# Two blocks of a transformer on one core: conditioning products as scaled row tiles on VectorE

## The chip, the core and the metric

The kernel runs on one core of a Trainium2 chip. The metric is the device time of one execution in microseconds (us). PE is TensorE, ACT is ScalarE, DVE is VectorE, SP is the engine whose queue issues nearly all transfers. Everything is in 32-bit floats.

## The reference, cut to what matters

Two models run one behind the other on 256 tokens of width 1024: first two layers (stick-breaking attention, dilated attention, feed-forward, a gated embedding), then two layers (MLA with pooling, GQA, a convolved feed-forward) that also see 256 context tokens. The second model is conditioned:

```
for i in range(2):
    ml = (silu(c) @ w_mod[i] + b_mod[i]).reshape(B, 6, 1, D)      # for the latents
    mc = (silu(c_ctx) @ w_mod[i] + b_mod[i]).reshape(6, D)        # for the context
    hl = modulate(xl, ml[:, 0], ml[:, 1]); hc = modulate(xc, mc[0], mc[1])
    ...                                                            # shifts, scales and gates 0 to 5
```

`w_mod` is 2 x 1024 x 6144, 50 MB: two vectors of 1024 times a matrix of 6144 columns, once for each layer. These products depend on `c` and `c_ctx` alone, so they can be made at any time before their use. The context leaves the kernel after layer 0, so of layer 1 its share is needed only for the first shift and scale (columns 0 to 2047).

## The kernel before, in words

**Linear layers.** Each is cut into weight chunks of at most 2048 elements a partition (1 MB), as a rule 8 blocks of 128 rows by 256 columns. There are 212 of them. A chunk is loaded by SP into one of three places of `raw`. ACT rounds it into `whi` (L1010, `split_high`), DVE makes the rest `wlo = raw - whi` (L1446, `split_low`), and PE adds three products: high by high, high by low, low by high (L647 is the line of every matmul). `whi` and `wlo` have three places (`SPLIT = 3`) too. So ACT may round chunk s+3 when PE has finished chunk s, DVE then makes its rest, and SP may load chunk s+6 into the place that this freed. Below, "the end of chunk s" is the time at which PE finishes it, and "position s" is the place in the order of ACT or DVE at which they handle the results of chunk s: evacuation, then the split of chunk s+3, then side work such as rotations (`rotate_pending`).

**Order of the linear layers.** `stick_qk` (8 chunks), `stick_v` (4), the attention phase `stick`, `stick_out` (4), `ff_in0` (16), `ff_out0` (16), `ple0`, `gate0`, then three times `dil_qk` (4) and `dil_v` (2), the phase `softmax`, `dil_out`, `ff_in1`, `ff_out1`, `ple1`, `gate1`; then with 512 tokens `mix_p`, `mix_c`, MLA, `mix_out`, `up00` (12), `down00` (8), `up01` (10), `down01` (8); then the second layer.

**The conditioning products.** `w_mod` is cut into 24 pieces of 512 columns by 1024 rows. A piece is two loads of 1 MB through the ring `raw`, without a split, in front of later chunks. PE makes `mod_products`: eight matmuls in full 32-bit with `cc` (the two vectors, as 2 of 24 columns, the others zero) as the fixed operand and 512 columns of the weights moving, four at a time in the four column groups of the array. The sums of a batch of up to 8 pieces gather in PSUM bank 7 (`MOD_BATCHES`). At the end of a batch ACT copies them (`mod_rows`, `modrow` lies in `lnv`), PE turns them with four matmuls (`mod_turn`), DVE adds the bias (`mod_keep`). The pieces stand in `stick_qk` (1), `stick` (7, one behind every second head), `mix_c` (2), `up00` (5), `down00` (3) and `up01` (6).

**Waits.** SP waits before each load for the user of the place's last content. A chunk whose last split is followed by a phase without matmul chunks can have that split put behind the phase (`late_splits`, `waiting_splits`), but not when the phase holds conditioning pieces.

Of the kernel before, what the change touches and what calls it, by code (L numbers as in the profile page):

```python
# [21 lines left out]
F32 = mybir.dt.float32  # L22
# [6 lines left out]
P = 128  # L29
D = 1024  # L30
# [19 lines left out]
MOD_ROWS = 24  # L50
MOD_BATCHES = (0, 8, 10, 12, 18, 24)
# [4 lines left out]
def constants():  # L56
# [20 lines left out]
    for q in range(4):  # L77
        for m in range(MOD_ROWS):
            select[32 * q + m, m] = 1.0
# [29 lines left out]
class Counting:  # L109
# [32 lines left out]
 ple_done max_ready fail_ready fail_summed stick_weights masked mod_rows mod_turned mod_kept gated_silu tiles_ready squares_folded half_moved""".split()  # L142


def build(nc, A, out, noted, dry_stop=None):
    C = Counting(noted)
    with ExitStack() as ctx:
        for f in FAMILIES:
            C.sems[f] = ctx.enter_context(nc.semaphore(f))
        landed = [ctx.enter_context(nc.semaphore(f"landed{i}")) for i in range(RAW)]  # L150
        loaded = {n: ctx.enter_context(nc.semaphore(f"loaded_{n}")) for n in ("squares", "rows", "freq", "pos", "x", "arena", "p")}
# [12 lines left out]
        h = sb("h", [P, KD, T2])  # L164
        u2 = sb("u2", [P, 2, KD, T2], F32R)
        uh, ul = u2[:, 0, :, :], u2[:, 1, :, :]
# [5 lines left out]
        cos1 = sb("cos1", [P, S])  # L172
        sin1 = sb("sin1", [P, S])
# [6 lines left out]
        cc = sb("cc", [P, KD, 2 * MOD_ROWS - 2])  # L180
        small = sb("small", [P, 64])
        ident, ones, negtri, negones, perm1, perm_m, perm_g, past, select = (squares[:, j, :] for j in range(9))
        select = select[:, 0:MOD_ROWS]
# [51 lines left out]
        pin, ph_, pl_ = y[:, 0:2, S:T2], uh[:, 0:2, S:T2], ul[:, 0:2, S:T2]  # L235
# [6 lines left out]
        csil = arena("csil", [P, 2, 512], 28 * K)  # L242

# [33 lines left out]
        for l in range(2):  # L277
# [3 lines left out]
            if l == 0:  # L281
# [3 lines left out]
                phase("stick", n_mods=7)  # L285
# [16 lines left out]
            linear(f"ple{l}", A["w_ple"][l], 2, [(0, D)], S, "ple", xin=("u", 0), tok0=S)  # L302
# [51 lines left out]
        mod_after = dict(stick_qk=(4,), mix_c=(0, 1), up00=(1, 3, 5, 7, 9), down00=(0, 1, 2), up01=(1, 2, 3, 5, 6, 7))  # L354
        own_chunks, behind, mod_n = [], {}, 0
        for p in phases:
            p["mods"] = {}
            places = range(p["n_mods"]) if "n_mods" in p else mod_after.get(p.get("name"), ())
            for g, grp in enumerate(p.get("groups", [()])):
                own_chunks += grp  # L360
                for place in places:
                    if "groups" in p and place != g:
                        continue
                    l, c = divmod(mod_n, 12)
                    pair = [dict(job=p, mod=(l, c, half), kn=4, C=512,
                                 src=A["w_mod_2"][l][half * 512:(half + 1) * 512, c * 512:(c + 1) * 512]) for half in range(2)]
                    behind.setdefault(len(own_chunks) + SPLIT - (2 if "groups" in p else 1), []).extend(pair)
                    p["mods"][place] = (mod_n, pair)
                    mod_n += 1
        assert mod_n == 24 or dry_stop is not None  # L370
        order = []
        for n, c in enumerate(own_chunks):
            order += [c] + behind.get(n, [])
        chunks = order
        n_split = 0
        for r, c in enumerate(chunks):
            c["r"] = r
            if "mod" not in c:
                c["s"] = n_split
                n_split += 1  # L380
        splits = [c for c in chunks if "s" in c]
# [1542 lines left out]
```

## Time and profile before

| | us |
|---|---|
| median of 3 runs (lowest, highest) | 1920.99 (1912.36, 1924.91) |
| the profiled execution: its own time | 1921.89 |
| the profiled execution: span | 1919.8 |
| PE busy in the span | 1820.7 |
| DVE busy | 1049.7 |
| ACT busy | 874.1 |
| mean granted clock of PE | 0.975 of full speed |
| loaded from memory | 262.08 MB |

The span is the time from the first to the last instruction; the kernel's own time holds 2.1 us more. A matmul's record has a modelled end, so the distance between starts says more than the duration. Records of full 32-bit matmuls come in two per matmul.

### The profile page before, as it was taken

To read this page: it belongs to the slowest core of one execution; us is meant where nothing else is said; L and a number is where in the kernel's file an instruction comes from. 1 tells how busy PE (TensorE), PEld (TensorE's weight loads), DVE (VectorE), ACT (ScalarE), POOL (GpSimd) and SP (SyncE) were. 2 spreads that over 40 slices of the span, in tenths; PEclk is the share of its full clock that TensorE was granted. 3 is DMA by queue.
4 is the path that set the end of the run, shared out by engine and by line. 5 is a ranking of instruction groups with operands and counts; after the bars stand their busy time and mean duration, and the time that the engine had idled before them with its cause. 6 is when DMAs were issued, how large, how long until landed. Compare 5 with 4: busy or idle time off the path is not lost.

```text
span 1919.8 us, 25364 instructions
## 1 busy us (share of the span) xinstructions
PE 1820.7 (95%) x10222; PEld 1496.4 (78%) x10222; DVE 1049.7 (55%) x1370; ACT 874.1 (46%) x1108; POOL 0.2 (0%) x4
## 2 busy tenths in 40 slices
PE   6989999989999899989988999999999988999998
PEld 4857788988887788887756686777877867789997
DVE  4444775466554776464456644444233555667764
ACT  5455454354435454345445625332222344565552
POOL 0000000000000000000000000000000000000000
PEclk9989999999989999999998999999999999999999
DMA  5766365534520456533313023544565224035551
GB/s 189 238 213 212 116 194 193 184 110 144 169 95 5 133 178 196 180 105 102 117 36 114 1 88 110 176 153 148 181 219 186 89 81 133 1 101 186 190 182 68
DMA packets 227895, 264.76 MB, mean 138 GB/s; under 512 B 4672, under 2 KB 196163, under 8 KB 227779
## 3 DMA queue, kind: packets, MB, share of 16 engines
q1 hardware_dynamic: 226114, 258.89, 41.1%
q10 hardware_dynamic: 1664, 4.26, 0.7%
q8 instruction: 81, 1.33, 0.3%
q14 instruction: 36, 0.29, 0.0%
HBM read 262.08 MB, written 1.05 MB: 137 GB/s over the span
## 4 chain that ended last, share of the span: by engine, by line
PE 83%; DVE 8%; ACT 7%; issue 1%; DMA 1%; DVEq 0%; ACTq 0%
PE ps L647 81%; ACT y L1267 2%; PE ps L944 2%; ACT u L1270 1%; DVE wlo L1446 1%; ACT whi L1010 1%; DVE y L1714 1%; DVE u L1707 1%; DVE y L1731 1%; DVE rstd L1629 1%; DVE rstd L1631 1%; DMA xin<-in_ctx 1%; DVE h L1735 0%; DVE h L1517 0%; ACT lnv L1085 0%
## 5 line engine op out<-in xcount | busy, mean ns | idle before, releaser
L647 PE MATMUL ps<-u,whi 128*128 128x512 f32 (+2 forms) x3408 | 896.8, 346 | 34.3 <-DVE u L1707 16.4
L647 PEld LDWEIGHTS ps<-u,whi 128*128 128x128 f32 (+1 forms) x3408 | 590.9, 191 | 141.5 <-DVE u L1707 26.0
L647 PE MATMUL ps<-u,wlo 128*128 128x256 f32 (+1 forms) x2084 | 645.6, 310 | 0.0
L1446 DVE TENSOR_TENSOR wlo<-raw,whi 128x2048 fp32r<-128x2048 f32 (+6 forms) x212 | 454.0, 2142 | 339.5 <-ACT whi L1010 335.6
L1010 ACT ACTIVATE whi<-raw 128x2048 fp32r<-128x2048 f32 (+6 forms) x212 | 380.7, 1796 | 230.2 <-PE ps L647 197.9
L647 PEld LDWEIGHTS ps<-u,wlo 128*128 128x128 f32 x2084 | 398.4, 191 | 20.9
L647 PE MATMUL ps<-hid,whi 128*128 128x512 f32 (+1 forms) x1212 | 352.6, 363 | 0.0
L647 PE MATMUL ps<-hid,wlo 128*128 128x256 f32 (+1 forms) x864 | 261.6, 303 | 0.0
L647 PEld LDWEIGHTS ps<-hid,whi 128*128 128x128 f32 x1212 | 216.4, 189 | 39.8 <-DVE y L1492 2.5
L647 PEld LDWEIGHTS ps<-hid,wlo 128*128 128x128 f32 x864 | 163.4, 189 | 6.9
L647 PE MATMUL ps<-squares 128*128 128x256 f32 (+1 forms) x396 | 95.0, 390 | 5.7 <-issue 3.2
L647 PEld LDWEIGHTS ps<-squares 128*128 128x128 f32 x396 | 76.3, 195 | 19.8 <-issue 9.6
L1192 ACT ACTIVATE cacc<-ps,convv 128x512 f32<-128x512 f32 (+1 forms) x44 | 29.6, 673 | 121.6 <-PE ps L647 120.8
L1536 DVE SCALAR_TENSOR_TENSOR cacc<-ps,convv,cacc 128x510 f32<-128x510 f32 (+1 forms) x44 | 27.1, 616 | 91.8 <-ACT cacc L1192 89.3
L647 PE MATMUL ps<-whi,u 128*128 128x512 f32 (+1 forms) x224 | 65.7, 374 | 0.0
L1202 ACT ACTIVATE csil<-cacc 128x512 f32<-128x512 f32 (+1 forms) x44 | 23.1, 525 | 91.1 <-PE ps L647 88.6
L1109 ACT ACTIVATE work<-ps 128x512 f32<-128x512 f32 x38 | 22.8, 599 | 90.3 <-PE ps L647 90.2
L1379 ACT ACTIVATE pt<-ps 128x512 f32<-128x512 f32 (+2 forms) x72 | 37.1, 515 | 53.4 <-PE ps L944 52.6
L1707 DVE TENSOR_TENSOR u<-y,u 128x256 fp32r<-128x256 f32 (+1 forms) x80 | 40.4, 505 | 26.5 <-ACT u L1270 21.5
L1549 DVE TENSOR_TENSOR csil<-ps,csil 128x512 f32<-128x512 f32 (+1 forms) x44 | 24.6, 559 | 51.9 <-ACT csil L1202 48.3
L944 PEld LDWEIGHTS ps<-squares,pr 128*128 128x128 f32 x232 | 28.8, 149 | 29.3 <-issue 15.6
L1270 ACT ACTIVATE u<-y 128x256 fp32r<-128x256 f32 (+1 forms) x80 | 38.5, 482 | 22.4 <-DVE y L1714 19.7
(211 smaller groups left out, 1578.7 us busy)
## 6 DMA issues: line engine op xcount, KB each, us to landing
raw<-in_w_mod SPq DMA_DIRECT2D x48, 1024.0 KB, 5.5
raw<-in_ffn_w_up SPq DMA_DIRECT2D x44, 1024.0 KB, 5.1
raw<-in_w_ff_in SPq DMA_DIRECT2D x32, 1024.0 KB, 5.3
raw<-in_w_ff_out SPq DMA_DIRECT2D x32, 1024.0 KB, 5.1
raw<-in_w_in_dil SPq DMA_DIRECT2D x18, 1024.0 KB, 5.1
raw<-in_w_in_sb SPq DMA_DIRECT2D x12, 1024.0 KB, 6.0
raw<-in_w_ple_gate SPq DMA_DIRECT2D x8, 1024.0 KB, 5.2
raw<-in_ffn_w_down SPq DMA_DIRECT2D x8, 896.0 KB, 5.0
```

What stands on the lines that cost most here:

```text
L647: return pe.matmul(out_, lhsT, rhs, start=start, stop=stop, skip_group_check=True)
L944: last = pe.transpose(ps[:, (4 + k // 4) if wide else 4 + n % 2, (k % 4) * P:(k % 4 + 1) * P], pr[:, n % 2, k * P:(k + 1) * P], ident)
L1010: nc.scalar.activation(whi[:, s % SPLIT, 0:n], raw[:, c["r"] % RAW, 0:n], ACT.Copy).then_inc(*up("weights_high", s))
L1192: nc.scalar.activation(cacc[:, j, 0:T], A_[:, j, :], ACT.Identity, bias=convv[:, l, 66 + f:67 + f], scale=convv[:, l, 22 + f:23 + f]).then ...
L1202: nc.scalar.activation(csil[:, j, 0:T], cacc[:, j, 0:T], ACT.Silu).then_inc(*up("gated_silu", (i, g - 1, j)))
L1267: nc.scalar.activation(y[:, k, sl], y[:, k, sl], ACT.Identity, bias=mod_at(l, which, k, s_), scale=mod_at(l, which + 1, k, s_)).then_inc(* ...
L1270: nc.scalar.activation(dst[:, k_, 0:p["T"]], y[:, p.get("s0", 0) + k, 0:p["T"]], ACT.Copy).then_inc(*up("operand_high", (i, k)))
L1379: nc.scalar.activation(pt[:, n % 2, c0:c0 + w], ps[:, (4 + c0 // 512) if u["mask"] is not None else 4 + n % 2, 0:w], ACT.Copy).then_inc(*u ...
L1446: nc.vector.tensor_tensor(wlo[:, s % SPLIT, 0:n], raw[:, c["r"] % RAW, 0:n], whi[:, s % SPLIT, 0:n].bitcast(F32), ALU.subtract).then_inc(* ...
L1536: nc.vector.scalar_tensor_tensor(a[:, :, 1:S], x[:, :, 0:S - 1], convv[:, l, f:f + 1], a[:, :, 1:S], ALU.mult, ALU.add).then_inc(*up("vect ...
L1549: nc.vector.tensor_tensor(csil[:, j, 0:T], A_[:, j, :], csil[:, j, 0:T], ALU.mult).then_inc(*up("group_read_v", (i, g, j)))
L1707: nc.vector.tensor_tensor((cl if c else ul)[:, k_, 0:T], y[:, s0 + k, 0:T], (ch if c else uh)[:, k_, 0:T].bitcast(F32), ALU.subtract).then ...
```

## The change

`w_mod` no longer goes through PE as a product. It is cut into 96 row tiles of 128 rows by 1024 columns (0.5 MB, two transfers of 256 KB each). DVE multiplies a tile by one number per partition (the entry of the vector for that row) and adds it to a running sum of 128 by 1024: `tensor_scalar` for the first of 8 tiles, `scalar_tensor_tensor` for the other seven, once for each vector. When the eight tiles of a set are in, PE adds the sum over its 128 partitions with a column of ones (`unit_row`), four matmuls of 512 columns in four column groups. ACT copies, PE turns, DVE adds the bias as before.

There are 10 sets: 0 to 7 have 1024 columns and both vectors (8 tiles, 16 DVE instructions each), 8 and 9 have 2048 columns and the first vector alone (16 tiles, 16 DVE instructions each). The tiles have five places of their own, three in the unused half of `u2` (sets 0 to 4) and two in the arena (sets 5 to 9); the ring `raw` now carries chunks alone, and `late_splits` no longer looks at pieces.

A planner places tiles by chunk (`share`). Worked out from its rules, the tiles lie at these positions of DVE, and PE adds the set behind the chunk named:

| set | tiles at positions | PE adds it behind chunk |
|---|---|---|
| 0 | 1 to 8 (`stick_qk`, first of `stick_v`), 1 each | 12 (`stick_out`) |
| 1 | 13, 14 (`stick_out`), 32 to 37 (`ff_out0`), 1 each | 38 |
| 2 | 39 to 43 (`ff_out0`), 53 to 55 (`dil_qk0`), 1 each | 56 |
| 3 | 57 to 64 (`dil_v0`, `dil_qk1`, `dil_v1`), 1 each | 65 (`dil_qk2`) |
| 4 | 66 to 70 (`dil_qk2`, `dil_v2`), 91 to 93 (`ff_out1`), 1 each | 94 |
| 5 | 130 to 133 (`up00`), 2 each | 134 |
| 6 | 135 to 138 (`up00`), 2 each | 139 |
| 7 | 140, 141 (`up00`), 142, 143 (`down00`), 2 each | 144 |
| 8 | 145 to 149 (`down00`), 150 to 152 (`up01`), 2 each | 153 |
| 9 | 154 to 159 (`up01`), 160, 161 (`down01`), 2 each | 162 |

The tile for a place is loaded by SP in front of the chunk load seven positions behind the place's last use, once DVE has taken the old tile. The turn stands two chunks behind the addition. The core of the diff:

```diff
@@ SP: loads
                 for c in chunks:
                     r = c["r"]
+                    for m in mod_dma.get(r, ()):
+                        if m["earlier"]:
+                            sp.wait_ge(*at("mod_taken", m["earlier"]["n"]))
+                        elif m["slot"] >= 3:
+                            sp.wait_ge(*at("attended", (mla_i, 31)))
+                        for unit in range(2):
+                            c0 = (m["c"] + unit) * 512
+                            src = A["w_mod_2"][m["set"]["l"]][m["k"] * P:(m["k"] + 1) * P, c0:c0 + 512]
+                            sp.dma_start(mod_weights(m)[:, 2 * unit:2 * unit + 2, :], src.rearrange("p (b c) -> p b c", b=2)).then_inc(mod_landed[m["slot"]], 16)
                     if r >= RAW:
-                        o = chunks[r - RAW]
-                        if "s" in o:
-                            sp.wait_ge(*at("weights_low", o["s"]))
-                        else:
-                            sp.wait_ge(*at("weights_used", ("mod", o["r"])))
+                        sp.wait_ge(*at("weights_low", r - RAW))
@@ PE: behind each chunk
-                    if g - 1 in p["mods"]:
-                        mod_turn(p["mods"][g - 1][0])
-                    if g in p["mods"]:
-                        mod_products(*p["mods"][g])
+                        mod_turn(c["r"] - 2)
+                        mod_products(c["r"])
...
+            def mod_products(r):
+                st = mod_place.get(r)
+                if st is None:
                     return
+                pe.wait_ge(*at("mod_taken", ("set", st["i"])))
+                for q in range(4):
+                    a, unit = (q % 2, q // 2) if len(st["vecs"]) == 2 else (q // 2, q % 2)
+                    last = mm(ps[32 * q:32 * q + 32, 7, :], unit_row[:, :], mod_sum(st, a)[:, 2 * unit:2 * unit + 2, :], True, True)
+                last.then_inc(*up("mod_added", st["i"]))
@@ DVE: behind the split of each position, ahead of the rotations
+            def mod_scaled(r):
+                for m in mod_steps.get(r, ()):
+                    k, st = m["k"], m["set"]
+                    if k == 0 and m["c"] == st["c0"] and st["i"] > 0:
+                        dve.wait_ge(*at("mod_added", st["i"] - 1))
+                    dve.wait_ge(mod_landed[m["slot"]], 32 * (m["nth"] + 1))
+                    for v in st["vecs"]:
+                        total = mod_sum(st, v if len(st["vecs"]) == 2 else (m["c"] - st["c0"]) // 2)
+                        dve.wait_ge(*own())
+                        if k == 0:
+                            nc.vector.tensor_scalar(total, mod_weights(m), cc[:, k, v:v + 1], None, ALU.mult).then_inc(*up("mod_taken", m["n"]))
+                        else:
+                            nc.vector.scalar_tensor_tensor(total, mod_weights(m), cc[:, k, v:v + 1], total, ALU.mult, ALU.add).then_inc(
+                                *up("mod_taken", m["n"]))
@@ late splits
-            if p["kind"] != "linear" or phases[p["i"] + 1]["kind"] in ("linear", "final", "dump") or phases[p["i"] + 1]["mods"]:
+            if p["kind"] != "linear" or phases[p["i"] + 1]["kind"] in ("linear", "final", "dump") :
                 return [], []
```

Beside this the embedding input `p` moves to other places (`pin0` and half of `rstd`, low part in `ul[:, 6:8]`), and the two rotation tables share one buffer.

## Rows read from the trace of the kernel before

**Rows 1.** Page: busy time by engine; the chain's shares by engine.
```profile
PE 1820.7 (95%) x10222; PEld 1496.4 (78%) x10222; DVE 1049.7 (55%) x1370; ACT 874.1 (46%) x1108; POOL 0.2 (0%) x4
...
PE 83%; DVE 8%; ACT 7%; issue 1%; DMA 1%; DVEq 0%; ACTq 0%
```
**Rows 2.** Waits: waiting line, releaser; us in total, times, longest.
```profile
PE ps L647 <- DVE u L1707: 16.4, 34, 3.2
```
**Rows 3.** Groups by form: xcount, busy us, mean ns, idle before; PE and DVE.
```profile
L647 PE MATMUL ps<-raw,cc 128*24 128x512 f32 x384 | 46.0, 597 | 0.0
...
L647 PE MATMUL ps<-squares,lnv 128*128 128x24 f32 x40 | 4.9, 261 | 0.0
...
L1446 DVE TENSOR_TENSOR wlo<-raw,whi 128x2048 fp32r<-128x2048 f32 x174 | 398.9, 2293 | 270.6 <-ACT whi L1010 267.8
...
L1714 DVE SCALAR_TENSOR_TENSOR y<-h,vec,rstd 128x256 f32<-128x256 f32 x48 | 23.3, 485 | 16.3 <-ACT rstd L1088 14.5 <-DVE wlo L1446 0.2
...
L1536 DVE SCALAR_TENSOR_TENSOR cacc<-ps,convv,cacc 128x510 f32<-128x510 f32 x22 | 16.5, 749 | 79.9 <-ACT cacc L1192 78.7
...
L1848 DVE TENSOR_SCALAR pr<-pr,small 128x512 f32<-128x512 f32 x32 | 15.6, 486 | 1.1
...
L1848 DVE TENSOR_SCALAR pr<-pr,small 128x768 f32<-128x768 f32 x8 | 5.0, 620 | 0.5 <-DVE small L1846 0.2
```
**Rows 4.** Timeline of PE in `up00`: start, us, operation.
```profile
1208.18 0.39 PE L647 MATMUL ps<-u,wlo 128*128 128x512 f32 x1
1208.50 1.92 PE L647 MATMUL ps<-raw,cc 128*24 128x512 f32 x16
1210.35 0.73 PE L647 MATMUL ps<-u,whi 128*128 128x512 f32 x2
```
**Rows 5.** Timeline of ACT in `stick`: one exponential per head.
```profile
129.48 0.49 ACT L1345 ACTIVATE sba<-ps 128x384 f32<-128x384 f32 x1 [1.84 <-PE ps L647]
132.19 0.49 ACT L1345 ACTIVATE sba<-ps 128x384 f32<-128x384 f32 x1 [0.47 <-PE ps L647]
136.75 0.49 ACT L1345 ACTIVATE sba<-ps 128x384 f32<-128x384 f32 x1 [1.84 <-PE ps L647]
```
**Rows 6.** Timeline of DVE and of PE at the start of `stick`.
```profile
107.80 2.29 DVE L1446 TENSOR_TENSOR wlo<-raw,whi 128x2048 fp32r<-128x2048 f32 x1 [4.23 <-ACT whi L1010]
...
111.27 2.08 PE L647 MATMUL ps<-sbf,squares 128*128 128x256 f32 x6 [3.83 <-DVE sbf L1788]
```
**Rows 7.** Windows: length, PE, PEld, DVE, ACT, POOL busy; clock, DMA share, GB/s.
```profile
108.00:112.00 4.00, 0.73 (x2) 0.64 (x3) 3.72 (x5) 2.93 (x6) 0.00 (x0) 0.50 0.18 28
...
144.00:152.00 8.00, 8.00 (x49) 4.86 (x49) 3.41 (x8) 5.04 (x11) 0.00 (x0) 1.00 0.86 300
```
**Rows 8.** Timeline of DVE in `ff_out0`: two splits in a row.
```profile
335.87 2.29 DVE L1446 TENSOR_TENSOR wlo<-raw,whi 128x2048 fp32r<-128x2048 f32 x1 [3.25 <-ACT whi L1010]
341.42 2.29 DVE L1446 TENSOR_TENSOR wlo<-raw,whi 128x2048 fp32r<-128x2048 f32 x1 [3.25 <-ACT whi L1010]
```
**Rows 9.** Timeline of DVE in `dil_qk0`, and at the start of its softmax.
```profile
471.13 2.29 DVE L1446 TENSOR_TENSOR wlo<-raw,whi 128x2048 fp32r<-128x2048 f32 x1 [2.07 <-ACT whi L1010]
473.52 0.69 DVE L1581 TENSOR_TENSOR work<-ps,sin 128x512 f32<-128x512 f32 x1
...
477.74 2.29 DVE L1446 TENSOR_TENSOR wlo<-raw,whi 128x2048 fp32r<-128x2048 f32 x1 [2.06 <-ACT whi L1010]
...
564.76 0.56 DVE L1831 CUSTOM_DVE_ANT_0 sm<-ps,masks 128x384 f32<-128x384 f32 x1 [5.29 <-PE ps L647]
```
**Rows 10.** Timeline of ACT and DVE in `up00`, behind an even chunk.
```profile
1197.73 1.60 ACT L1192 ACTIVATE cacc<-ps,convv 128x512 f32<-128x512 f32 x2 [9.37 <-PE ps L647]
...
1203.41 2.29 DVE L1446 TENSOR_TENSOR wlo<-raw,whi 128x2048 fp32r<-128x2048 f32 x1
```
**Rows 11.** Transfers by line: count, KB each, median us to landing.
```profile
raw<-in_w_mod SPq DMA_DIRECT2D x48, 1024.0 KB, 5.5
...
ropeg<-in_const_rope ACTq DMA_DIRECT2D x1, 256.0 KB, 2.8
```

More of the change, by code:

```diff
@@ L350, in build @@
                 p["idle"] = 11 if phases[i - 1]["T"] == T2 else 7
[L354 to L375, printed above, removed]
-        for r, c in enumerate(chunks):
[L377 to L381, printed above, removed]
+        for r, c in enumerate(chunks):
+            c["r"] = c["s"] = r
+        mla_i = max((i for i, p in enumerate(phases) if p.get("what") == "mla"), default=None)
@@ new lines, in jobs_at, with unbroken @@
+        def jobs_at(name):
+            return min((c["r"] for c in chunks if c["job"]["name"] == name), default=len(chunks))
+        def unbroken(p, q):
+            between = phases[p["i"]:q["i"]]
+            return all(o["kind"] == "linear" and "stat" not in o for o in between)
+        sets = []
+        for a, b in [(n, n + 2) for n in range(0, 16, 2)] + [(16, 20), (20, 24)]:
+            sets.append(dict(i=len(sets), l=a // 12, c0=a % 12, c1=a % 12 + b - a, vecs=(0, 1) if b - a == 2 else (0,)))
@@ new lines, in build @@
+        share = dict(stick_qk=1, stick_v=2, stick_out=1, ff_out0=2, dil_qk0=1, dil_v0=1, dil_qk1=1, dil_v1=1,
+                     dil_qk2=1, dil_v2=1, ff_out1=2, up00=4, down00=4, up01=4, down01=4)
+        mod_steps, mod_place, mod_dma, mod_tiles = {}, {}, {}, []
+        todo = [(st, c, k) for st in sets for c in range(st["c0"], st["c1"], 2) for k in range(KD)]
+        free_at, early = 1, 0
+        for ck in chunks:
+            r, job = ck["r"], ck["job"]
+            room = share.get(job["name"], 0)
+            if job.get("stat") and ck["g"] + 1 == len(job["groups"]):
+                room = 0
+            while room > 0 and todo and r >= free_at and (todo[0][0]["i"] < 5) == (r < jobs_at("mix_p")):
+                st, c, k = todo[0]
+                n = len(mod_tiles)
+                early += st["i"] < 5
+                slot = n % 3 if st["i"] < 5 else 3 + (n - early) % 2
+                earlier = [m for m in mod_tiles if m["slot"] == slot]
+                if earlier and earlier[-1]["r"] == r:
+                    break
+                todo.pop(0)
+                m = dict(n=n, set=st, c=c, k=k, slot=slot, nth=len(earlier), earlier=earlier[-1] if earlier else None, r=r)
+                mod_tiles.append(m)
+                mod_steps.setdefault(r, []).append(m)
+                mod_dma.setdefault((earlier[-1]["r"] if earlier else r - 3) + 7, []).append(m)
+                room -= len(st["vecs"])
+                if not todo or todo[0][0] is not st:
+                    place = r + 1
+                    while place + 3 < len(chunks) and not unbroken(chunks[place]["job"], chunks[place + 3]["job"]):
+                        place += 1
+                    mod_place[place] = st
+                    free_at = place + 1
@@ L385, in build @@
+        assert not todo or dry_stop is not None
+        splits = chunks
         for p in phases:
@@ L632, in build @@
             if p.get("name", "").startswith("ff_in"):
-                p["loads"] = [(pin[:, :, :], A["p"][int(p["name"][5:]), 0].rearrange("(t p) d -> p t d", p=P))]
+                p["loads"] = [(pin[t], A["p"][int(p["name"][5:]), 0][t * P:(t + 1) * P, :]) for t in range(2)]
             for _ in p.get("loads", ()):
```

130 lines of the change are left out of this document (64 added, 66 removed).

## The prediction

> **What bounds the kernel now.** I read the page first: PE is busy 1820.7 of 1919.8 us and makes 83% of the chain that ended last; DVE is busy 55% of the span [rows 1]. Then the waits: the longest wait of PE's matmuls in total is 16 us, on the first operand tiles of a layer, not on weights [rows 2]. So in the linear layers every us taken off PE's queue is a us of the span, and VectorE has slack on average. But PE, ACT and DVE are coupled at every chunk, so the question is where DVE is late once it carries the tiles. The profiled execution took 1921.9 us, 0.9 over the median of 1921.0; all sums are against it. A difference under 1% (19 us) can't be told from no change here.
>
> **What leaves PE.** The 24 pieces make 46 us of PE in all [rows 3]. In `up00` a piece starts at 1208.50, and the next chunk's matmul starts 2.17 us after the last one of the chunk before [rows 4]. A chunk is 48 matmuls in 10.7 us (from 1197.73, where ACT is released by its predecessor [rows 10], to the piece's start less a matmul), 0.22 each; so the piece costs 1.94 us. 17 pieces stand in linear layers: **-33.0**. The turns: 40 records, 4.9 us, five turns, about 0.9 us of path each [rows 3]; four are in linear layers: **-3.6**.
>
> Seven pieces are in `stick`. A head that has no piece ahead of it takes 132.19-129.48 = 2.71 us, one that has takes 4.56 [rows 5]. The difference, 1.85, is nearly the whole piece, but ACT had only 0.47 us of idle in the short head, so when all heads are short ACT is nearly the bound as well; 1.83 each: **-12.8**. The fifth turn and its `mod_keep` stand between the last two heads: **-1.0**. And `stick` no longer holds pieces, so the split of chunk 14 goes behind it: DVE's 2.29 us of it end at 110.09, and PE starts the first head's sums at 111.27 after 3.83 us of waiting for DVE [rows 6]: **-2.3**. Behind `stick` that split is hidden by chunks 12 and 13; without that cover it costs 4 us. The clock fell to 0.50 in that wait [rows 7]. A shorter wait may keep it: a gain between 0 and 2.5 us (five or six short heads of matmuls at half speed), taken as 0, since PE still waits.
>
> **What comes to PE.** Ten additions of four matmuls where a piece had eight: half of 1.94, say 1.0, and ten turns of 0.9: **+19**. Ten ACT copies of 0.6 us for five, and twice the small `mod_keep`, lie in slack: 0. Without waits the sum is -33.7.
>
> **What comes to DVE.** A multiply-add with a per-partition number took 485 ns for 256 and 749 ns for 510 elements, so 1.04 ns an element and, as an estimate, 1.28 us for 1024. `tensor_scalar` took 486 and 620 ns for 512 and 768: 0.75 us for 1024 [rows 3]. 140 of the first and 20 of the second: 195 us, DVE to 65%. A tile for both vectors is 2.65 us with gaps. The Trainium skill, VectorE: DVE Perf Modes, section on the fixed extra latency, gives (N+151)/0.96 for a plain tensor-tensor, 1.22 us here; its rule would shorten the waits below by some 10%, and leaves the forecast where it is.
>
> Now each addition. PE reaches it one chunk after the last tile's position began. DVE begins there with the split of three chunks ahead, for which ACT must first round.
> - `ff_out0`, `ff_out1`: splits are 5.55 us apart, and DVE idles 3.25 us between them [rows 8]. The split begins 2.0 us after the chunk's end (ACT's rounding), ends at 4.3, the tile at 6.95; PE is there at 5.55. Sets 1 and 4 wait 1.4 each: **+2.8**.
> - `dil_qk`: chunks end 6.6 us apart; DVE has 2.29 of split and three rotations of 0.73 [rows 9], with a tile 7.15 us. DVE falls behind by 0.55 each time, beyond the wait for ACT of about 2.9 us that starts every position. Set 2 (three positions, the first without rotation): DVE ends at 476.6, PE is there at 474.85: **+1.75**. Set 3 has eight positions in a row. Following them one by one (split when ACT is ready or DVE free, tile, rotation of the chunk before) DVE ends 4.5 us after chunk 65: **+4.5**. That is a stop as long as the one that lost the clock at 108 us [rows 7]; half speed for 4 us costs **+2**.
> - Set 4's five positions lead up to the dilated softmax. DVE's first instruction of it is at 564.76, after 5.29 us of idle [rows 9]. With two rotations, five tiles (one of them short) and the splits moved along, DVE is free at 567.9: **+3.2**.
> - Tiles at 13 and 14 delay the last copy of `stick_out`, on which the norm waits: **+1.2**.
> - `up00`, two tiles of 5.3 us: an even chunk's DVE work ran to 8.0 us behind the chunk's end (1203.41+2.29-1197.73 [rows 10]), with tiles 13.3, where the next chunk ends at 10.8. The odd one has some 3 us less and gives part of it back. Followed chunk by chunk the ends lie 0.9 (set 5), 2.4 (set 6) and, into the shorter chunks of `down00`, 3.1 us (set 7) behind PE: **+6.4**. Sets 8 and 9 have half the DVE work: 0 and **+0.75**. Set 0: two phases of time, 0.
> The split itself (`wlo`) is never late: it has three chunks of lead, 16 us, and DVE lags at most 5.
>
> **Transfers.** The same 50 MB go in 192 transfers of 256 KB past the chunk loads on SP's queue. SP waits for `mod_taken` before each tile; the load queued behind it waits for a split that DVE makes later than that tile, so the wait costs nothing. In `ff_out0` and `stick_qk` a chunk and a tile, 1.57 MB, must come in 5.55 us: 283 GB/s. `stick` moved 300 GB/s for 8 us with PE never idle [rows 7]. Cost 0, with the second rival as the bound. The moves of `p` and of the tables: 0, the same work in other places, hidden under `ff_out`; uncovered 3 us.
>
> **Sum.** -33.7 + 2.8 + 1.75 + 4.5 + 2 + 3.2 + 1.2 + 6.4 + 0.75 = -11.1: 1921.9 - 11.1 = **1911 us**. The gain is two thirds eaten by PE waiting for DVE.
>
> **Rivals.**
> - *DVE is in time.* If a multiply-add is cheaper than I extrapolate, or the lags don't add up, only the -33.7 remains: 1888; with the clock kept at 108 us, 1886. For it: three chunks of lead, DVE at 65%. Against it: PE stands at the addition without any lead, one chunk after the last tile, and the 1.4 us in `ff_out0` need no lag. It decides from a tile below 1.3 us. Chance 0.25.
> - *The transfers bind; slower.* A 1 MB load lands in 5.5 us (190 GB/s alone), 256 KB in 2.8 us, half the time for a quarter of the bytes [rows 11]. Place: the 40 early positions with a tile. If no more than 230 GB/s come through, 1.57 MB take 6.8 us: 24 positions of 5.55 us lose 1.3, 16 of 6.6 lose 0.2, together +34: 1945. At 190 GB/s it is 24 x 2.7 + 16 x 1.65 = +91: 2002. It decides below 283 GB/s. Against it: 300 GB/s in `stick`, in loads of 1 MB. Chance 0.11. The Trainium skill, DMA: Bandwidth & Descriptors, section Bandwidth, asks for transfers of 1 MiB or more for three quarters of the peak (341 GB/s at 1 MB, 138 at 64 KB); by that rule the change goes this way.
> - *The pieces filled time that is lost anyway* (ACT's order in `stick`, waits that move elsewhere), and DVE's lags also delay evacuations: gain under 5 us, 1917 to 1930. Chance 0.19.
> - Forecast, 1902 to 1917: 0.45.
>
> **Range.** 1889 to 1929 leaves out the transfers' case and the far end of the first rival. The likeliest case's own range is 1902 to 1917. Faster by over 1% means below 1902: the first rival and the low edge of the forecast, 0.32. Slower than 1940: the transfers and a little of the third, 0.12. Within: 0.56.
>
> **What would show it.** The profile after should show about 80 records of additions (128 x 32) where 384 of `raw`,`cc` stood, DVE's multiply-adds at 1.28 us x140, DVE near 1245 us; a wait of PE on them of 15 us in all, the longest at `dil_qk2` about 4 to 5 us, and a clock dip there; `stick` shorter by 16 us, all heads at 2.7; the first split at `stick`'s start gone. No wait of DVE on a tile's transfer. I am wrong if PE's wait on DVE there is under 5 us (first rival), or if DVE or ACT wait on DMA for more than 10 us (second).

## The result: same at 2%, on the slow side, and the forecast was for faster

The changed kernel took **1928.86 us** (median of 20, 1919.06 to 1944.23), the kernel before 1920.53 (20 runs, 1912.0 to 1927.34): ratio 1.0057, 95% interval 1.0033 to 1.0081. Forecast was 1911. Eight more executions, in a second comparison, gave 1.0069 (1.0038 to 1.0099). The profiled execution, 1943.85 us (span 1942.0), is one of the slowest; two later profiled ones had spans of 1921.3 and 1937.0, so three traces of each kernel are used below. The median of all 29 executions of the changed kernel is 1930.95 us. One of the twelve executions of before_fill_more took 2412.84 us at a mean granted clock of 0.70; it is left out of that run's ratio.

The page of the changed kernel, then the matmuls' waits on VectorE, answering [rows 1, 2]; columns as there.

```profile
PE 1816.4 (94%) x9958; PEld 1509.7 (78%) x9958; DVE 1245.1 (64%) x1539; ACT 877.2 (45%) x1113; POOL 0.2 (0%) x4
...
PE 72%; DVE 16%; ACT 8%; issue 2%; DMA 1%; DVEq 0%; ACTq 0%; SPq 0%
```
```profile
PE ps L685 <- DVE u L1756: 16.5, 35, 3.2
...
PE ps L685 <- DVE y L1695: 9.6, 4, 4.7
PE ps L685 <- DVE work L1695: 6.9, 3, 3.1
...
PE ps L685 <- DVE small L1878: 4.3, 1, 4.3
```

TensorE lost its 24 pieces and is busy only 4 us less; VectorE's share of the chain doubled. The three new lines are the waits for the sets' sums (L1695) and for VectorE at the start of the dilated softmax. A fourth, 2.2 us, stands at the last set. The new work by form, answering [rows 3]:

```profile
L1695 DVE SCALAR_TENSOR_TENSOR y<-idle_half,cc,y 128x1024 f32<-128x1024 f32 x70 | 89.9, 1284 | 4.9
...
L1693 DVE TENSOR_SCALAR y<-idle_half,cc 128x1024 f32<-128x1024 f32 x10 | 7.5, 753 | 0.8
```
```profile
L685 PE MATMUL ps<-squares,lnv 128*128 128x4 f32 x80 | 9.5, 242 | 0.0
...
L685 PE MATMUL ps<-y,unit_row 128*32 128x512 f32 x40 | 7.1, 786 | 9.6 <-DVE y L1695 9.6
```

1.28 us and 0.75 us, as extrapolated. The two splits of `ff_out0` [rows 8] now have a tile between them, and the first addition behind comes late, TensorE's line third:

```profile
333.02 2.29 DVE L1476 TENSOR_TENSOR wlo<-raw,whi 128x2048 fp32r<-128x2048 f32 x1 [0.54 <-ACT whi L1041]
335.42 2.60 DVE L1695 SCALAR_TENSOR_TENSOR y<-idle_half,cc,y 128x1024 f32<-128x1024 f32 x2
338.66 2.29 DVE L1476 TENSOR_TENSOR wlo<-raw,whi 128x2048 fp32r<-128x2048 f32 x1 [0.64 <-ACT whi L1041]
```
```profile
338.07 1.06 PE L685 MATMUL ps<-y,unit_row 128*32 128x512 f32 x8 [1.45 <-DVE y L1695]
...
544.54 1.93 PE L685 MATMUL ps<-y,unit_row 128*32 128x512 f32 x8 [4.66 <-DVE y L1695]
...
586.51 2.07 PE L685 MATMUL ps<-qk 64*128 64x256 f32 x4 [4.29 <-DVE small L1878]
```

The second line is set 3, the third the dilated softmax. There VectorE still worked off tiles when its first maximum was due, where it had idled 5.29 us [rows 9]:

```profile
580.40 5.31 DVE L1695 SCALAR_TENSOR_TENSOR y<-idle_half,cc,y 128x1024 f32<-128x1024 f32 x4
585.89 0.56 DVE L1878 CUSTOM_DVE_ANT_0 sm<-ps,masks 128x384 f32<-128x384 f32 x1 [0.18 <-DVE y L1695]
```

At the sticks the wait is down from 3.83 to 2.09 us [rows 6], but the exponentials [rows 5] show the first heads 3.58, 5.05 and 3.49 us apart and only the later ones at the forecast 2.7, by turns 2.84 and 2.59. (The kernel before had 3.58, 5.24 and 2.72 there: its first heads were as long.)

```profile
108.70 1.65 PE L685 MATMUL ps<-sbf,squares 128*128 128x256 f32 x4 [2.09 <-DVE sbf L1839]
```
```profile
110.81 0.49 ACT L1377 ACTIVATE sba<-ps 128x384 f32<-128x384 f32 x1 [1.52 <-PE ps L685]
114.39 0.49 ACT L1377 ACTIVATE sba<-ps 128x384 f32<-128x384 f32 x1 [1.34 <-PE ps L685]
119.44 0.49 ACT L1377 ACTIVATE sba<-ps 128x384 f32<-128x384 f32 x1 [2.81 <-PE ps L685]
122.93 0.49 ACT L1377 ACTIVATE sba<-ps 128x384 f32<-128x384 f32 x1 [1.25 <-PE ps L685]
125.77 0.49 ACT L1377 ACTIVATE sba<-ps 128x384 f32<-128x384 f32 x1
```

The windows say why (columns as in [rows 7]; the granted clock follows POOL): sticks, the norm behind `stick_out`, dilated softmax, latent attention. The second fence is the kernel before at the same work.

```profile
108.00:124.00 16.00, 15.30 (x50) 11.11 (x51) 6.24 (x14) 8.19 (x18) 0.00 (x0) 0.59 0.00 1
184.00:200.00 16.00, 11.73 (x39) 9.19 (x38) 10.30 (x20) 4.04 (x7) 0.00 (x0) 0.79 0.28 91
...
580.00:612.00 32.00, 26.72 (x115) 20.15 (x116) 16.37 (x41) 10.93 (x24) 0.00 (x0) 0.68 0.16 50
1052.00:1088.00 36.00, 34.82 (x105) 21.51 (x105) 18.76 (x66) 14.25 (x45) 0.00 (x0) 0.53 0.06 21
```
```profile
108.00:124.00 16.00, 12.73 (x55) 8.48 (x56) 7.30 (x12) 8.57 (x18) 0.00 (x0) 0.68 0.40 137
564.00:596.00 32.00, 31.46 (x166) 23.71 (x165) 15.09 (x48) 14.65 (x33) 0.00 (x0) 0.79 0.00 1
1028.00:1064.00 36.00, 34.18 (x135) 20.67 (x136) 24.45 (x78) 19.30 (x57) 0.00 (x0) 0.76 0.12 40
```

With the levels 2.4 and 1.2 GHz, a mean clock of c over a window of T us holds (1-c)/0.5 x T us at half clock: 20.5 us in the changed kernel's softmax against 13.4, 33.8 in its latent attention against 17.3. Over the whole span (mean clocks 0.961, 0.971, 0.961 against 0.975, 0.975, 0.976) it is 151, 111 and 151 us against 96, 96 and 92.

The extra half clock is not spread evenly. Read in windows of 1 us and summed by the stages of the table below, it is (mean of three traces, changed against before): start to `stick_out` 15.9 against 15.9 us, join 4.6 against 0, dilated stages 27.3 against 12.5, latent attention 29.6 against 15.9, `up00` to `down01` 11.0 against 0.7. The other stages differ by under 3 us each.

The transfers did no harm (count, KB, median us to landing, answering [rows 11]); in the whole trace VectorE waited 2.0 us for a tile.

```profile
modw<-in_w_mod SPq DMA_DIRECT2D x112, 256.0 KB, 4.0
idle_half<-in_w_mod SPq DMA_DIRECT2D x80, 256.0 KB, 3.4
```

**Where the time went.** Stage lengths between the records of ScalarE that write `rstd` (us). First column: the kernel before, mean of three traces; the others are differences to it. "Changed" is the mean of three traces, the experiments one trace each.

| stage | before | forecast | changed | fill | add_later | combined_mla | before_all_fill |
|---|---|---|---|---|---|---|---|
| start to stick_out, its norm | 171.4 | -14.9 | -10.5 | -15.0 | -11.1 | -16.4 | -4.9 |
| join | 9.9 | 0 | +1.6 | 0.0 | +2.5 | 0.0 | 0.0 |
| ff_in0, ff_out0 | 188.7 | +3.3 | +5.0 | +5.2 | +3.3 | +1.0 | +1.7 |
| ple0, gate0, norms | 52.0 | 0 | +1.0 | +0.2 | +1.1 | +0.2 | +1.5 |
| dilated stages | 188.9 | +15.3 | +20.4 | +10.1 | +13.3 | +2.7 | -3.6 |
| join, ff_in1, ff_out1 | 205.8 | +3.3 | +1.9 | +1.8 | +0.4 | +2.3 | +0.5 |
| to mix_c | 142.7 | -4.8 | -3.9 | -3.6 | -5.1 | -3.0 | 0.0 |
| latent attention, mix_out | 168.0 | 0 | +5.9 | +9.4 | +0.6 | -3.4 | -4.5 |
| up00 to down01 | 410.0 | -13.2 | -7.4 | -8.8 | -21.6 | -20.6 | -0.3 |
| rest | 345.2 | 0 | -0.7 | -0.9 | -0.3 | -0.9 | -0.8 |
| sum | 1882.7 | -11 | +13.3 | -1.5 | -16.8 | -38.0 | -10.4 |

The forecast's column is its terms put to their stages (an addition with its turn 1.9, a piece -1.94, waits as listed). The miss by these traces is 24 us, by the medians 18. fill's and before_fill_more's traces have the long stretch in the latent attention told of below, so their sums lie above their medians. The miss sits in the sticks with the norm behind them and the join (6), the dilated stages (5), the latent attention (6, code that the change does not touch) and `up00` to `down01` (6).

### The profile page after: what moved, and what is told of

Same layout as the page of the kernel before. It is cut to its first block, busy times and chain, and to the rows that moved or that the text cites. A ratio compares the mean times of both kernels' runs of the same rounds, so it can differ in the third digit from the quotient of the medians.

```text
span 1942.0 us, 25257 instructions
## 1 busy us (share of the span) xinstructions
PE 1816.4 (94%) x9958; PEld 1509.7 (78%) x9958; DVE 1245.1 (64%) x1539; ACT 877.2 (45%) x1113; POOL 0.2 (0%) x4
## 4 chain that ended last, share of the span: by engine, by line
PE 72%; DVE 16%; ACT 8%; issue 2%; DMA 1%; DVEq 0%; ACTq 0%; SPq 0%
PE ps L685 70%; DVE wlo L1476 4%; DVE y L1695 2%; ACT y L1299 2%; ACT whi L1041 2%; PE ps L975 2%; ACT u L1302 1%; DVE work L1695 1%; DVE sq L1695 1%; DVE y L1763 1%; DVE u L1756 1%; DVE rstd L1659 1%; DVE rstd L1661 1%; DMA xin<-in_ctx 1%; DVE h L1547 0%
## 5 line engine op out<-in xcount | busy, mean ns | idle before, releaser
L685 PEld LDWEIGHTS ps<-squares 128*128 128x128 f32 x396 | 78.5, 201 | 20.4 <-issue 9.1
L1695 DVE SCALAR_TENSOR_TENSOR y<-idle_half,cc,y 128x1024 f32<-128x1024 f32 x70 | 89.9, 1284 | 4.9
L1223 ACT ACTIVATE cacc<-ps,convv 128x512 f32<-128x512 f32 (+1 forms) x44 | 29.6, 673 | 113.3 <-PE ps L685 112.5
L1566 DVE SCALAR_TENSOR_TENSOR cacc<-ps,convv,cacc 128x510 f32<-128x510 f32 (+1 forms) x44 | 27.1, 616 | 50.2 <-ACT cacc L1223 47.5
L685 PE MATMUL ps<-sq,squares 128*128 128x256 f32 (+1 forms) x108 | 39.6, 494 | 9.7 <-DVE qg L1622 6.1
```

The source lines that it names most:

```text
L685: return pe.matmul(out_, lhsT, rhs, start=start, stop=stop, skip_group_check=True)
L1223: nc.scalar.activation(cacc[:, j, 0:T], A_[:, j, :], ACT.Identity, bias=convv[:, l, 66 + f:67 + f], scale=convv[:, l, 22 + f:23 + f]).then ...
L1566: nc.vector.scalar_tensor_tensor(a[:, :, 1:S], x[:, :, 0:S - 1], convv[:, l, f:f + 1], a[:, :, 1:S], ALU.mult, ALU.add).then_inc(*up("vect ...
L1695: nc.vector.scalar_tensor_tensor(total, mod_weights(m), cc[:, k, v:v + 1], total, ALU.mult, ALU.add).then_inc(*up("mod_taken", m["n"]))
```

## The experiments

**Theory.** The waits for VectorE came as forecast; what was mis-sized is TensorE's clock: behind idle time of 2 to 5 us at the stage ends and additions it falls to half, and 3 to 34 us of work follow at that speed. **Rivals:** the waits alone are the loss; or the clock is luck.

**Both kernels again** (no edit).

> The kernel before, unchanged, profiled a second time. Question: how much of the change in the low-clock time between the two traces (before 0.975 of the span at full clock, after 0.961) is chance. Every theory: time 1.000 of before. Clock theory (gaps that VectorE makes at stage ends let TensorE's clock fall): the low-clock stretches of this kernel repeat, with none at the third set's place (dil_qk2) and the dilated softmax at full clock again by 580 us; mean clock 0.973 to 0.977. Chance theory (the low stretches in the changed kernel are luck): a stretch that the first profile did not have turns up here too, and the mean clock differs from 0.975 by over 0.005.

> The changed kernel, unchanged, profiled a second time. Every theory: 1.004 of before. Clock theory: clock below 0.9 again at 540 to 550 us (third set's addition) and at 580 to 610 us (start of the dilated softmax), behind waits of TensorE of over 2 us for VectorE, and 8 us of half clock more than in the kernel before behind the sticks. Whatever low stretch it does not show again, the latent attention's from 1052 to 1086 us above all, is chance and no part of the loss. Chance theory: the low stretches sit elsewhere.

> The kernel before a third time: half clock in the latent attention for 17.1 and 13.7 us in the first two. If its length is luck with the same odds in both kernels, a stretch of over 20 us should be seen in about one of three executions; if not, it stays at 13 to 17 us and the changed kernel loses there for a reason of its own.

> The changed kernel a third time, for one more trace of the latent attention, code that the change does not touch: half clock there for 34.1 and 10.2 us in the first two. If its length is luck, it lies between 10 and 34 us, and the rest of the trace agrees with the other two within 3 us in every stretch.

Measured: before_again 1921.45 us, ratio 0.9999 (0.9977 to 1.0022), mean clock 0.975; after_again 1932.27 us, 1.0069 (1.0038 to 1.0099), profiled at 0.971; before_third 1923.83, after_third 1938.82 (one execution each). Behind the third set and in the dilated softmax there was half clock in all three traces of the changed kernel, and the softmax's stretch was 17 to 21 us against 10 to 14 before. That is not luck. The latent attention is another matter; its windows in after_again and after_third:

```profile
1040.00:1076.00 36.00, 32.39 (x141) 19.60 (x139) 26.08 (x78) 20.90 (x58) 0.00 (x0) 0.86 0.18 59
```
```profile
1040.00:1076.00 36.00, 32.61 (x101) 20.19 (x101) 20.88 (x62) 16.18 (x44) 0.00 (x0) 0.59 0.18 59
```

0.86 and 0.59 are 10 and 30 us at half clock in the window at the same instructions behind the same waits. That stage's length differs by 10.4 us between the three traces, the largest part of why the changed kernel's executions lie 25 us apart; the rest agreed within 4.5 us in each stage (3 was expected), the most in the sticks and in `up00` to `down01`. The kernel before showed 17, 14 and 14.

**fill**: TensorE kept busy ahead of its waits, VectorE's work and moments untouched.

```
+ fill(n): n matmuls ones x squares, 256 columns, into a bank nobody reads
  mod_products:        + fill({1: 3, 2: 4, 3: 10, 6: 5, 7: 6}.get(set, 0)) ahead of the wait
  sticks, first head:  + fill(4)
  behind stick_out:    - idle(5)  + idle(12)
  dilated softmax:     + fill(9) ahead of the third scores
```

> The changed kernel with matmuls that nobody reads put ahead of the waits for VectorE: 3, 4, 10, 5 and 6 ahead of the additions of sets 1, 2, 3, 6, 7, 9 at the start of the dilated softmax, 4 at the first head of the sticks, and 12 in place of 5 behind stick_out. VectorE's work and the moment at which its results come are untouched; TensorE is only busy instead of idle before them. Clock theory: the clock stays at full speed behind the third set and in the dilated softmax, and the low stretch behind the sticks is shorter: 8 to 17 us less than the changed kernel, 0.995 to 1.000 of before. Rival (the waits themselves are the whole loss, the clock is chance): no change from the changed kernel or up to 2 us more, 1.004 to 1.005.

Measured: 1912.16 us, 0.9961 (0.9939 to 0.9982), 20.1 us less than after_again's 1932.27 in the same comparison, 16.7 less than the first comparison's 1928.86. Its sticks, set 3 and dilated softmax ran at full clock:

```profile
104.00:120.00 16.00, 14.94 (x80) 11.60 (x81) 6.81 (x15) 12.43 (x25) 0.00 (x0) 1.00 0.19 63
...
540.00:548.00 8.00, 8.00 (x65) 7.52 (x63) 3.17 (x3) 3.20 (x4) 0.00 (x0) 1.00 0.01 2
568.00:600.00 32.00, 30.28 (x190) 23.69 (x190) 21.34 (x55) 16.17 (x35) 0.00 (x0) 1.00 0.16 50
```

From the first `q,k` matmul to the last exponential the sticks took 44.3 us, where the changed kernel needed 50.0, 49.1 and 47.5. The table puts 10 of the gain in the dilated stages, 4.5 in the sticks, 1.6 in the join. In `up00` to `down01` the fillers gave 1.4 us, though half clock there went from 11.0 to 6.6 us: most of the loss in that stretch was the waits themselves, and there the rival is right.

**add_later**: the additions one chunk further behind.

```
  if last tile of the set:  place = r + 1 (moved on to an unbroken place)
+     if place == r + 1:
+         place += 1      (and moved on in the same way)
```

> The changed kernel with TensorE's four additions of each set one chunk later, so that VectorE, which ends a set's last tile late, has a whole chunk more; tiles and loads stay where they are. The waits of TensorE for the sets' sums (9.6 us in all, largest 4.66 at the third set) should go to under 1 us. Clock theory: the waits and the clock dips behind them both go, 11 to 16 us less than the changed kernel, so 0.995 to 0.999 of before; the slow stretch at the dilated softmax's start stays, since VectorE is late there for its tiles and not for the addition. Rival (VectorE's backlog only moves on: TensorE waits for the operand or the split instead): 0 to 4 us less, 1.002 to 1.004 of before, and the wait stands at another line at the same time.

Measured: 1907.41 us, **0.992** (0.989 to 0.9951), 25 us under after_again (21 under the first comparison's median) and more than either theory gave. No wait of TensorE for L1695's sums is left in its trace; the other waits that grew did so by 1.8 us in all, 1.1 of them for `qk`. `up00` to `down01` is 21.6 us shorter than before; the forecast without its waits says 13.2+7.15 = 20.4. The softmax's wait stayed, as expected:

```profile
576.13 2.50 PE L689 MATMUL ps<-qk 64*128 64x256 f32 x5 [4.61 <-DVE small L1882]
```

**tiles_off_dil_v2**: on top of add_later.

```
- dil_v2=1
+ dil_v2=0
```

> The kernel add_later with the two tiles (four passes of VectorE, 5.1 us) of dil_v2 moved into ff_out1, the share of dil_v2 set to 0. Term tested: the start of the dilated softmax, priced +3.2 us, where TensorE now waits 4.6 us for VectorE and then runs 17 to 20 us at half clock against 10 to 14 in the kernel before. VectorE-backlog theory: the wait is back at 0.4 to 0.6 us and the half clock at 10 to 14 us, 5 to 9 us less than add_later: 0.987 to 0.990 of before. Rival (the four additions and turns moved in front of the softmax make it late, not the tiles): the wait stays over 3 us, and 0.991 to 0.993.

Measured: 1897.1 us, 0.9867 (0.9836 to 0.9898), 10 us under add_later, of which its trace shows 4.7 in the dilated stages. What the rest is, its trace, the slowest of its six executions, does not show. The wait came of the tiles, not of the additions:

```profile
570.05 1.41 PE L689 MATMUL ps<-qk 64*128 64x256 f32 x4 [0.43 <-DVE small L1882]
```

The half clock behind stayed at 17 us, longer than the 10 to 14 expected.

**before_stick_fill and before_fill_more**: the same fillers in the kernel before.

```
  sticks, first head:  + fill(4)          (before_fill_more: + fill(8))
  dilated softmax:     (before_fill_more: + fill(3) ahead of the scores, + fill(1) ahead of the third)
```

> The kernel BEFORE, with only four matmuls that nobody reads at the first head of the sticks, where TensorE waits 3.83 us for VectorE (rows 6). It asks whether the 5.6 us that the fillers brought in the changed kernel's sticks belong to the change at all. Clock theory (the half clock for 10.2 us from 108 us on is set by that idle time, in either kernel): no low stretch at 108 to 124 us, the sticks 4 to 6 us shorter, 0.997 to 0.998 of before. Rival (only the changed kernel loses clock there): no change, 0.9995 to 1.001.

> The kernel BEFORE with eight unread matmuls at the first head (four left 1.91 us of idle and a half clock of 6.8 us), and 3 and 1 of them at the start of the dilated softmax, in front of the waits of 1.21 and 0.43 us. It asks what the fillers alone bring to the kernel before, and so what part of combined's gain is not of the moved products. Clock theory: no half clock at 108 to 124 us and at 565 to 590 us; the sticks' part from 58.2 us to 55 to 57, the softmax from 46.8 us to 43 to 45: 4 to 7 us less, 0.9965 to 0.998 of before. Rival (in the kernel before the heads and the softmax are bound by other engines even at half clock): 0 to 2 us, 0.999 to 1.001.

Measured: before_stick_fill 1923.04 us, 1.0007 (0.999 to 1.0024). The theory's gain did not come, but the test is inconclusive: four fillers left a wait of 1.91 us in front of the first sums, and the clock fell as before, for 7 us instead of 10.

```profile
108.59 1.99 PE L647 MATMUL ps<-squares 128*128 128x256 f32 x8
112.50 1.70 PE L647 MATMUL ps<-sbf,squares 128*128 128x256 f32 x6 [1.91 <-DVE sbf L1795]
```

before_fill_more: 1920.32 us, 0.9988 (0.9969 to 1.0007), less than expected. In its trace the sticks ran at full clock and took 57.7 us instead of 61.0, 61.7 and 61.2; the dilated stages were 3.7 us shorter. But most of what it gained there this trace lost in the latent attention (5.9 us), where the kernel before now had 31 us of half clock too (windows of the sticks and of the latent attention):

```profile
106.00:122.00 16.00, 15.15 (x87) 11.03 (x88) 7.52 (x13) 11.61 (x20) 0.00 (x0) 1.00 0.61 212
...
1020.00:1056.00 36.00, 33.02 (x104) 20.45 (x103) 21.38 (x63) 15.67 (x45) 0.00 (x0) 0.57 0.18 59
```

So the long stretch does not need the moved products. The sticks at full clock, first and last exponential, in before_fill_more and then in fill (51.2 and 39.5 us):

```profile
113.22 0.49 ACT L1356 ACTIVATE sba<-ps 128x384 f32<-128x384 f32 x1 [1.28 <-PE ps L647]
...
164.38 0.49 ACT L1356 ACTIVATE sba<-ps 128x384 f32<-128x384 f32 x1 [0.69 <-PE ps L647]
```
```profile
109.70 0.49 ACT L1387 ACTIVATE sba<-ps 128x384 f32<-128x384 f32 x1 [0.59 <-PE ps L685]
...
149.20 0.49 ACT L1387 ACTIVATE sba<-ps 128x384 f32<-128x384 f32 x1 [1.68 <-PE ps L685]
```

**after_mla_fill**, **combined** and **combined_mla**.

```
after_mla_fill (on the changed kernel):
  pool_w:          + fill(3)
  latent softmax:  + fill(4) ahead of the first scores
combined (on tiles_off_dil_v2): the two above, sticks + fill(4), behind stick_out idle(12),
  dilated softmax + fill(3) ahead of the scores, + fill(1) ahead of the third
combined_mla (on combined): pool_w - fill(3); latent softmax fill(4) becomes fill(5),
  + fill(4) ahead of the first turn, + fill(2) ahead of the second
```

> The changed kernel with matmuls that nobody reads only in the latent attention: 3 ahead of the pool's weights and 4 ahead of the first scores, in front of waits of 1.6 and 2.1 us that both kernels have. The changed kernel's executions lie anywhere from 1919 to 1944 us, the kernel before's only from 1912 to 1930; in one trace of the changed kernel the clock stood at half for 34 us from 1053 us on, in another for 10 us at 1046. Theory: this stretch is the spread, and it is chance, given by the same idle time in both kernels: with the fillers the low stretch is 0 to 3.4 us, no execution is over 1932, the median is 1920 to 1925, 0.9995 to 1.002 of before. Rival (the spread comes from elsewhere, from the changed kernel's own waits): the median stays at 1927 to 1932 and the spread over 20 us.

> All together: the additions one chunk later, no tiles in dil_v2, and matmuls that nobody reads ahead of the waits at the first head (4), behind stick_out (12 in place of 5), ahead of the dilated softmax (3 and 1), of the pool's weights (3) and of the latent scores (4). Clock theory, summed from the parts: add_later 1907.4, less 7 for dil_v2's tiles, 5.6 for the sticks, 1.5 for the join, 5 for the dilated softmax's clock, 6 for the latent attention's: 1882, 0.978 to 0.984 of before. Rival (a stretch held at full clock lets the next one fall instead, so that the parts do not add up): 1890 to 1900, 0.985 to 0.990.

> combined without the 3 matmuls ahead of the pool's weights (the wait of 1.62 us stood there as before), but with 5 ahead of the first latent scores and 4 and 2 ahead of the first two turns, where TensorE waited 1.39 and 0.53 us. Theory: the half clock in the latent attention (10 to 34 us long in every trace so far) is set at these waits, and goes: 5 to 9 us less than combined, 1882 to 1886, 0.980 to 0.981 of before. Rival (it comes of the few columns per us that TensorE has in this softmax, not of the idle before): it stays over 10 us, 1889 to 1895, 0.984.

Measured: after_mla_fill 1934.89 us, 1.0063 (1.0042 to 1.0085). The theory missed: the half clock stayed, 31 us. Without fillers the clock falls within the first scores, behind waits of 1.63 and 2.1 us; here the scores ran at full clock, and it fell behind the next wait, ahead of the first turn:

```profile
1045.55 0.44 PE L982 MATMUL ps<-squares,pr 128*128 128x128 f32 x2 [1.39 <-DVE pr L1905]
```

combined: 1890.89 us, 0.9839 (0.9813 to 0.9866): the parts add up to within 9 us of the 1882 summed, which is the theory's range by the ratio and the rival's by the microseconds. No half clock turned up in another stage; the latent attention kept 20 us of it, as it had 24 in tiles_off_dil_v2. combined_mla put fillers ahead of the two turns, and one more ahead of the scores: **1882.81 us, 0.9799** (0.9772 to 0.9827), and that half clock was gone. The step between units of the latent attention in after_mla_fill at half clock, then in combined_mla (same operation, start in the first column):

```profile
1048.61 1.22 PE L685 MATMUL ps<-km,qm 96*128 96x256 f32 x2
...
1051.24 1.22 PE L685 MATMUL ps<-km,qm 96*128 96x256 f32 x2
```
```profile
1025.31 0.70 PE L689 MATMUL ps<-km,qm 96*128 96x256 f32 x2
...
1026.74 0.70 PE L689 MATMUL ps<-km,qm 96*128 96x256 f32 x2
```

2.63 us a unit against 1.43. Idle times of 0.5 to 2.1 us ahead of the scores and the first turns decide over 10 to 34 us.

**after_mla_turns and before_all_fill.**

```
after_mla_turns (on the changed kernel): latent softmax + fill(5), + fill(4), + fill(2)
before_all_fill (on before_fill_more):   latent softmax + fill(5), + fill(4), + fill(2)
```

> The changed kernel with unread matmuls in the latent attention alone: 5 ahead of the first scores, 4 and 2 ahead of the first two turns, which took away that half clock in combined_mla. Luck theory (of the loss against the forecast, half is a stretch of half clock in untouched code that lasts 34 us in most executions of the changed kernel and 14 to 17 in the kernel before): no half clock there, its stretch 164 to 165 us instead of 167 to 178, the median of 1930 falls to 1917 to 1921 and the spread under 12 us; 0.998 to 1.000 of before. Rival (only the waits and the dips of the changed stages count): 1925 to 1929, 1.003 or more.

> The kernel BEFORE with the fillers of combined_mla: 8 at the first head, 3 and 1 at the dilated softmax, 5 ahead of the first latent scores, 4 and 2 ahead of the first two turns. It is the ground against which combined_mla tells what the moved products are worth with neither waits nor lost clock, a term that the prediction put at -33.7 us. Theory: before_fill_more (0.9988) less 3 to 8 us for the latent attention's half clock: 1911 to 1916, 0.995 to 0.998 of before; the products then are worth 28 to 33 us. Rival (the fillers brought most of combined_mla's gain): 1895 or less, 0.987.

Measured: after_mla_turns 1923.22 us, 1.0007 (0.9993 to 1.0022), between the two expectations; all but one of 12 executions within 6 us. Half clock in its window (0.53 to 0.86 without fillers):

```profile
1040.00:1076.00 36.00, 33.47 (x165) 22.14 (x165) 27.98 (x77) 23.10 (x60) 0.00 (x0) 1.00 0.25 83
```

So the latent attention's clock cost the changed kernel 0.5 to 0.6% (1.0057 and 1.0069 less 1.0007), 10 to 12 us, of which the kernel before pays a part too: before_all_fill, 1911.77 us, 0.994 (0.9919 to 0.9962), is 8.6 us under before_fill_more, and its trace shows that stage 4.5 us under the usual one.

before_all_fill against combined_mla: both have the fillers, neither has waits for the moved products. 1911.77-1882.81 = **29.0 us** is what moving the products is worth when VectorE is given time for it. The two were measured in different comparisons; by their ratios to the kernel before (0.994 and 0.9799) it is 27 us, by the table's sums 27.6. Half clock is the same in both, 58 and 60 us in the traces. Forecast: -33.7.

## Why the prediction was wrong, step by step

- **The forecast and the sign.** The measured 1928.86 us lies just inside the stated 1889 to 1929, but on the other side of the kernel before: +8.3 us by the medians where -11.1 was forecast, 19.4 too much. Three terms share it: the gain (4.7 us too large), the waits (4.6 too small) and the clock (the rest, 10).
- **What leaves PE, what comes to it (-33.7).** Too large by 5 to 7 us: 29.0 or 27. In `up00` to `down01`, combined_mla against before_all_fill is -20.3, forecast -20.4. In the sticks, with full clock on both sides, it is 44.3 against 57.7 us, -13.4, where the forecast had -12.8, -1.0 and -2.3, 16.1 in all (the two kernels as they are: 48.9 against 61.3, -12.4). The wait for the split got shorter by 1.7 us and not 2.3. The exponentials, first to last, took 39.5 us against 51.2, a gain of 11.7 where 13.8 was forecast: five of the pieces gave 1.86 us each and a sixth 1.8, as read, but the last piece and the turn together only 0.6, since the last two heads were short before (3.72 and 1.87 us). The dilated stages are short by 2.5 us more (+6.3 for two additions, forecast +3.8).
- **What comes to DVE.** Right: 1245.1 us busy, 1.28 and 0.75 us. The Trainium skill, VectorE: DVE Perf Modes, in its section on the fixed extra latency, led to an estimate of 1.22 us for such an operation as a plain tensor-tensor; the trace has 1.284 and decides.
- **Waits at the additions (16.2).** Right in kind and nearly in size: 18.7 us. Set by set 1.45, 1.90, 4.66, 1.54 for sets 1 to 4 (forecast 1.4, 1.75, 4.5, 1.4), 1.16, 2.64, 3.07 for 5 to 7 (0.9, 2.4, 3.1), 2.25 for the last (0.75; there two tiles came 1 us late).
- **Late softmax (+3.2) and norm (+1.2).** Too small: the waits grew by 3.9 (4.29 from 0.43) and 2.6 us (3.2 from 0.6). With the additions, all waits came to 25.2 us against 20.6.
- **The clock: the step that failed.** It is the largest of the three errors. The forecast priced "half speed for 4 us costs +2" behind set 3, took the sticks' clock "as 0", and gave nothing to the other waits. Behind set 3 it was right: 3.4, 6.8 and 6.8 us of half clock, so at most 1.7 to 3.4 us lost. In the start up to `stick_out` it was right too: 15.9 us at half clock in both kernels, 4.6 us over the full-clock 44.3 now and 3.6 over the 57.7 before. What it left out are the waits at the join, at the dilated softmax, at sets 6, 7 and 9, and the latent attention. Half clock went from 95 to 138 us a run (means of three), 43 us more. TensorE's work takes about twice as long in it (the four matmuls of an addition 1.93 us against 1.06), so at most half of it is lost, 21 us. What it really cost is what is left when the gain and the waits are taken off: +8.3+29.0-25.2 = 12 us by the medians, 13.3+27.6-25.2 = 16 by the traces, where +2 stood. fill shows the cause: with VectorE's work left as it was and TensorE kept busy ahead of its waits it was 17 to 20 us faster, a part of which the same fillers would have brought in the kernel before. By place: the dilated stages 5 over the forecast (fill took 10 away, before_fill_more 3.7), the latent attention 6, the join 1.6, and behind sets 6, 7 and 9 a part that was not separated (at most 5 by the half clock, 1.4 by fill). The row for it was there [rows 7]: I read half clock in the 4 us of the wait, and not that it lasted 10 us in all, seven of them behind the wait.
- **Untouched code at 0.** Wrong on average by 6 us. That this stretch hangs on TensorE's short idle times ahead of the first scores and the first turns is shown by the three kernels with fillers at both, which have none; which of these waits is enough was not separated. Why it was long (31 to 34 us) in four traces of five of the changed kernel, after_mla_fill and fill, and in none of three of the kernel before, is open: it can be chance or an effect of what runs ahead. before_fill_more had it too, so the moved products are not needed for it.
- **Transfers (0; rival 0.11).** Nearly right: 2.0 us of waits in all, in set 9, whose sum came 1.5 us later than forecast. The Trainium skill, DMA: Bandwidth & Descriptors, section Bandwidth, wants 1 MiB a transfer; here 256 KB at a time beside the 1 MB loads landed in 3.4 and 4.0 us (medians) and cost no more than those 2.0 us, so the trace does not bear out a loss from it at this load.
- **Rivals.** "DVE in time" needed a tile under 1.3 us with its wait gone; waits were all there. Nearest was the third, "the pieces filled time that is lost anyway" (1917 to 1930): right number, wrong mechanism. The time was not lost anyway; 27 to 29 us were won and given back as waits (25 us) and as half clock (12 to 16).

## What to carry to other kernels

When work moves off the bounding engine, give its consumer a lead (here one chunk, worth 21 to 25 us) and keep the moved work away from the stages where the helper engine is the one waited for (10 us). Price a wait of TensorE not by its length but by what runs behind it at half clock: read the granted clock in windows until it is back at 1.00, and ask whether the work there is TensorE's. Where such a wait can't be removed, matmuls into an unused bank ahead of it can be worth more than the wait, in the kernel before too (0.994).

## What the runs showed of the hardware that was not expected

- In the latent attention 10 to 34 us at 1.2 GHz followed waits of TensorE of 1.63 and 2.1 us ahead of the first scores, or, where these were filled (after_mla_fill), of 1.39 us ahead of the first turn; the length differed between executions of one kernel (34, 10 and 34 us). With TensorE busy ahead of the scores and the turns the clock stayed at 2.4 GHz. The Trainium skill, TensorE: Matmul & The Clock Gate, section on HAM oscillation, tells of kernels whose clock swings between the two levels because TensorE idles between groups of matmuls; the traces agree.
- Chunks of the same code ran at two paces, a split every 5.55 us or every 5.65. All three traces of the changed kernel have 5.65 in `ff_in0` and 5.55 in `ff_in1`. Two of the kernel before have it the other way round, but before_third has it like the changed kernel, and before_all_fill has 5.65 in both. So the pace is not fixed by the kernel, and 16 chunks can differ by 1.6 us for no reason of the change. The cause was not looked for.
